# Neighbourhood attention: the values computed with tokens on partitions, four pairs of heads at a time, and the input rounded in column order

## What is computed

```python
for i in range(DEPTH_2):                       # 4 layers
    h = rmsnorm(x, norm1_g[i])
    ...                                        # i == 1: y = nat_mixer(h, ...)
    x = x + y
    h = rmsnorm(x, norm2_g[i])
    x = x + conv_ffn(h, ...)

def nat_mixer(h, w_qkv, q_g, k_g, rpb, w_out):
    rows = s // GRID_W                         # 512 tokens = 8 rows of 64 columns
    qkv = (h @ w_qkv).reshape(b, s, 3, NAT_HEADS, NAT_HEAD_DIM)   # 16 heads of 64
    q = rmsnorm(qkv[:, :, 0], q_g) * (NAT_HEAD_DIM ** -0.5)
    k = rmsnorm(qkv[:, :, 1], k_g)
    v = qkv[:, :, 2]
    # each token attends to all 8 rows of the 16 columns around its own
    ...
    sc = einsum(q, k_win) + bias
    p = softmax(sc)
    out = einsum(p, v_win)
    return out @ w_out
```

## Time and profile before

| | us |
|---|---|
| median of 3 runs | 3117.59 |
| lowest and highest | 3113.52, 3118.71 |
| the profiled execution, its own time | 3118.01 |
| its span in the trace | 3116.2 |
| PE busy in it | 3090.2 |
| POOL, DVE, ACT busy | 1495.0, 1412.7, 1268.6 |

### The profile page before, as it was taken

The page is one execution under the profiler, slowest core; times in us unless marked ns, Lnnn a source line. Parts: engine busy times, 40 slices in busy tenths (PEclk is TensorE's granted clock), DMA queues, the critical chain, the costliest instruction groups (busy, mean ns, idle before and its releaser), DMA issues.

```text
span 3116.2 us, 35743 instructions
## 1 busy us (share of the span) xinstructions
PE 3090.2 (99%) x14233; PEld 2461.1 (79%) x14233; DVE 1412.7 (45%) x2644; ACT 1268.6 (41%) x1973; POOL 1495.0 (48%) x732
## 2 busy tenths in 40 slices
PE   9999999999999999999999999999999999999999
PEld 6768888875888887778888888888888887588887
DVE  6564111288533345445343544423534358763433
ACT  5463222266433335554333333323433337643432
POOL 2225545566454453334554534444454557545554
PEclk9999999999999999999999999999999999999999
DMA  5213333344232333222323322222333335423332
GB/s 191 71 51 92 96 98 97 96 123 128 82 101 94 95 101 105 92 83 94 102 88 101 108 76 80 81 82 75 94 102 95 95 98 136 112 90 102 91 98 88
DMA packets 90038, 302.78 MB, mean 97 GB/s; under 512 B 10000, under 2 KB 10512, under 8 KB 89744
## 3 DMA queue, kind: packets, MB, share of 16 engines
q1 hardware_dynamic: 89152, 299.35, 31.6%
q10 hardware_dynamic: 720, 1.14, 0.1%
HBM read 281.07 MB, written 2.10 MB: 91 GB/s over the span
## 4 chain that ended last, share of the span: by engine, by line
PE 89%; DVE 7%; ACT 2%; DMA 1%; issue 1%; SPq 0%; ACTq 0%; DVEq 0%
PE PS L1492 26%; PE PS L1494 26%; PE PS L1493 26%; PE PS L1701 1%; DVE XH L2129 1%; DVE XL L2131 1%; PE PS L1515 1%; PE PS L1505 1%; PE PS L1506 1%; PE PS L1504 1%; DMA PT<-PD 1%; PE PS L1519 1%; DVE X L2157 1%; DVE PS L2434 1%; PE PS L1571 1%
## 5 line engine op out<-in xcount | busy, mean ns | idle before, releaser
L2597 POOL TENSOR_TENSOR WL<-RAW,WH 128x1024 fp32r<-128x1024 f32 x502 | 1209.6, 2411 | 1236.1 <-ACT WH L1812 1235.8
L1492 PE MATMUL PS<-XH,WH 128*128 128x512 f32 x2632 | 1054.1, 400 | 2.8 <-POOL WL L2597 1.3
L1494 PE MATMUL PS<-XH,WL 128*128 128x512 f32 x2632 | 1027.2, 390 | 0.0
L1493 PE MATMUL PS<-XL,WH 128*128 128x512 f32 x2632 | 1026.8, 390 | 0.0
L1812 ACT ACTIVATE WH<-RAW 128x1024 fp32r<-128x1024 f32 x502 | 527.5, 1051 | 445.5 <-PE PS L1494 433.4
L1492 PEld LDWEIGHTS PS<-XH,WH 128*128 128x128 f32 x2632 | 494.7, 188 | 139.1 <-issue 36.5
L1493 PEld LDWEIGHTS PS<-XL,WH 128*128 128x128 f32 x2632 | 495.1, 188 | 106.6 <-issue 8.9
L1494 PEld LDWEIGHTS PS<-XH,WL 128*128 128x128 f32 x2632 | 494.8, 188 | 104.5
L1492 PE MATMUL PS<-HH,WH 128*128 128x512 f32 x1264 | 495.1, 392 | 4.4 <-DVE HL L2477 4.4
L1494 PE MATMUL PS<-HH,WL 128*128 128x512 f32 x1264 | 493.6, 391 | 0.0
L1493 PE MATMUL PS<-HL,WH 128*128 128x512 f32 x1264 | 493.5, 390 | 0.0
(11 more groups left out here) (278 smaller groups left out, 2378.4 us busy)
## 6 DMA issues: line engine op xcount, KB each, us to landing
RAW<-wst SPq DMA_DIRECT2D x502, 512.0 KB, 3.5
PT<-PD SPq DMA_DIRECT2D x36, 260.0 KB, 4.9
BI<-natb SPq DMA_DIRECT2D x16, 384.0 KB, 4.4
PT<-PD SPq DMA_DIRECT2D x16, 258.0 KB, 4.9
X<-xin SPq DMA_DIRECT2D x16, 256.0 KB, 5.0
PT<-PD SPq DMA_DIRECT2D x8, 262.0 KB, 4.8
X<-cmpw SPq DMA_DIRECT2D x1, 2048.0 KB, 8.1
out<-X SPq DMA_DIRECT2D x8, 256.0 KB, 2.0
```

The lines of the kernel that those rows point to most:

```text
L1492: e.matmul(o, wh, h, start=first, stop=False)
L1493: e.matmul(o, wh, l, start=False, stop=False)
L1494: t = e.matmul(o, wl, h, start=False, stop=last)
L2597: e.tensor_tensor(WL[:, b % NSPLIT, :], RAW[:, b % NRAW, :], WH[:, b % NSPLIT, :].bitcast(f32), SUB).then_inc(*did(lo_made, ("lo", b)))
```

## The change

Three things change in the program.

1. The weights of the attention's first product are stored in another order: v of four pairs of heads, then q and k of these four, then the same for the other four. v is made by `by_tokens` straight with tokens on partitions (8 input chunks times 4 token blocks, twice). DVE scales the four results by 1/rms, which is now a number per partition (`nat_tokens`); these numbers come from 1/rms by 4 transposes once (`rs_tokens`). The three blocks shifted by 64 are put together by two transfers each inside SBUF, 12 transfers in all. The transposes of v and their ACT copies are gone, as is the strided read in `scaled`.
2. For layer 1, `norm_chunk` puts the tokens in column order when it rounds x: it reads X with a stride of 64 numbers, on DVE for XH and XL and on ACT for the square, and writes in order.
3. `norm_stats` is now a queued piece of work, due 8 tiles into the first product. The beats are due 9, 12, 15, 18 and 21 tiles after k. Scores and probabilities lie in PT, not in TT.

```diff
-            out.append(("nat_qkv", 8, 24))
+            for half in range(2):
+                out.append((f"nat_v{half}", 8, 4))
+                out.append((f"nat_qk{half}", 8, 8))
...
-                turned = Ring([PT[:, i, j, :] for i in range(2) for j in range(4)], (*pt_free[0], *pt_free[1]))
+                spread = Ring([PT[:, 0, j, :] for j in range(4)], pt_free[0])
+                turned = Ring([PT[:, 1, j, :] for j in range(4)], pt_free[1])
+                rt = G8[:, 4:8]
+
+                def start():
+                    norm_stats(norm)
+
+                    def turn():
+                        bank = banks.get()
+                        i = step("rs_tokens", norm["rs"].ap, norm["rs_made"], rt, bank.ap, bank.free)
+                        bank.done((i, "rt"))
+                        st["rt"] = (i, "rt")
+                    later(turn, 6, first=True)
+
+                def to_values(t, bank, made):
+                    v = tiles.get()
+                    i = step("nat_tokens", v.ap, bank.ap, rt[:, t:t + 1], (made, st["rt"], *v.free))
+                    bank.done((i, "v"))
+                    cur["v0"].append((v, (i, "v")))
+                    if t == 0:
+                        return
+                    s = tiles.get()
+                    (above, above_made), (below, below_made) = cur["v0"][t - 1:t + 1]
+                    event = ("shifted", cur["half"])
+                    fetch(s.ap[0:64, :], above.ap[64:128, :], shift_in, event, above_made, *s.free)
+                    fetch(s.ap[64:128, :], below.ap[0:64, :], shift_in, event, below_made)
+                    cur["v1"].append(s)
...
-                    i = step("scaled", columns(b.ap), by_column(bank.ap), by_column(norm["rs"].ap),
-                             (made, norm["rs_made"], *b.free))
-                    bank.done((i, "z"))
-                    norm["z"] = z = (i, "z")
+                    norm["z"] = z = scaled(b.ap, bank, norm, made, b.free)
...
-                    def go():
-                        tokens(b.ap, 4, v0)
-                        b.done((tokens(b.ap[:, 64:448], 3, v1), "tr"))
-                    later(go, first=True)
...
-                        ss = tiles.get(), tiles.get()
+                        ss = spread.get(), spread.get()
...
-                        later(beat(n), 4 + 4 * n)
-
-                linear(norm["mv"], 24, evac, mid=lambda: norm_stats(norm), pace=1)
+                        later(beat(n), 9 + 3 * n)
+
+                for half in range(2):
+                    if half == 0:
+                        later(start, 8, first=True)
+                    cur.update(half=half, v0=[], v1=[])
+                    by_tokens(norm["mv"], to_values)
+                    linear(norm["mv"], 8, evac, pace=1, room=4)
...
-            def norm_chunk(i, k, gain, x_made, s, s_free, sq, total):
-                x = X[:, k, :]
+            def norm_chunk(i, k, by_col, gain, x_made, s, s_free, sq, total):
+                x, xh, xl = X[:, k, :], XH[:, k, :], XL[:, k, :]
+                if by_col:
+                    x, xh, xl = by_column(x), columns(xh), columns(xl)
...
-                e.tensor_scalar(XH[:, k, :], x, gain, None, MUL).then_inc(*did(dve_made, (i, "hi")))
+                e.tensor_scalar(xh, x, gain, None, MUL).then_inc(*did(dve_made, (i, "hi")))
...
+            def nat_tokens(i, v, bank, scale, after):
+                for event in after:
+                    w.wait_ge(*at(event))
+                e.tensor_scalar(v, bank, scale, None, MUL).then_inc(*did(dve_made, (i, "v")))
```

More of the change, by code:

```diff
@@ L1233, in evac @@
                                   *slot_free[h % 4])
-                    if kind < 2:
-                        cur[kind] = (b, head_norm(b, z, G8[:, 2:3] if kind == 0 else pcol("nat_k")))
+                    cur[kind] = (b, head_norm(b, z, G8[:, 2:3] if kind == 0 else pcol("nat_k")))
+                    if kind == 0:
                         return
-                    v0, v1 = tiles.get(), tiles.get()
-                    toks = []
-                    def tokens(src, n, dst):
-                        bank = banks.get()
-                        i = step("to_tokens", src, n, z, dst.ap, dst.free, bank.ap, bank.free)
-                        bank.done((i, "tok"))
-                        toks.append((i, "tok"))
-                        return i
-                    def go():
-                        tokens(b.ap, 4, v0)
-                        b.done((tokens(b.ap[:, 64:448], 3, v1), "tr"))
-                    later(go, first=True)
                     (q, qt), (k, kt) = cur[0], cur[1]
+                    v0, v1 = [x for x, _ in cur["v0"]], cur["v1"]
+                    v_made = (*(x for _, x in cur["v0"]), ("shifted", cur["half"]))
                     flight = {}
-                    blocks = [(v0, 0), (v0, 1)], [(v1, 0), (v1, 1)], [(v1, 1), (v1, 2)], [(v0, 2), (v0, 3)]
+                    blocks = (v0[0], v0[1]), (v1[0], v1[1]), (v1[1], v1[2]), (v0[2], v0[3])
                     def scores(n):
@@ L1479, in walk @@
                     bias_free = ret_layer(norm, n2, bias_free)
-                norm = new_norm("norm1", 8 * (layer + 1)) if layer < 3 else None
+                norm = new_norm("norm1", 8 * (layer + 1), layer == 0) if layer < 3 else None
                 ffn(n2, norm, layer, final=layer == 3)
@@ L1822, in norm_chunk @@
                     w.wait_ge(*at(event))
[L1823 removed]
+                e.activation(columns(s) if by_col else s, by_column(X[:, k, :]) if by_col else X[:, k, :],
+                             ACT.Square).then_inc(*did(act_made, (i, "sq")))
             def first_chunk(i, k, gain, x_in):
@@ L2750 @@
     w = g["nat_w_qkv_2"][0]
-    W["nat_qkv"] = w.reshape(D, 3, 8, 128).transpose(0, 2, 1, 3).reshape(D, 3072)
+    for half in range(2):
+        part = w.reshape(D, 3, 8, 128)[:, :, 4 * half:4 * half + 4]
+        W[f"nat_v{half}"] = part[:, 2].reshape(D, 512)
+        W[f"nat_qk{half}"] = part[:, 0:2].transpose(0, 2, 1, 3).reshape(D, 1024)
     W["nat_out"] = g["nat_w_out_2"][0]
```

32 lines of the change are left out of this document (19 added, 13 removed).

## The result

The changed kernel takes 3136.6 us (median of 6 runs, 3134.7 to 3138.2); the kernel before, in six runs beside it, 3114.9 (3112.9 to 3118.7). The ratio is 1.0066, with a 95% interval from 1.0055 to 1.0077: slower by 21.7 us, where +3.6 was forecast and the range ended at 3128.5. Between the two profiled executions it is 20.2 us (spans of 3136.4 and 3116.2).

A forecast was written before the change was run, and what follows sets the result against it. PE, busy 99% of the span, was taken to bound the kernel. Terms: -5.65 - 0.27 + 6.8 + 1.2 + 1.5 = +3.6 us, so 3121.2 us, range 3114.0 to 3128.5.

The forecast's parts named there:

- Turns, -5.65 us: PE in layer 1: 56 transposes of v go (6.1 us), four for `rs_tokens` come in (0.44 us).
- the 0.27 us for XL of chunk 7: PE's last macs of the first output chunk: the old wait for XL goes, -0.27 us.
- Strided reads, +0.59 us a chunk: DVE's layer 1 norm: XH 0.20 and XL 0.39 us longer, +4.7 us for eight chunks, range 0 to 7.7.
- strides cost nothing: Rival at layer 1's norm, 15%: chain ends at 1185.5, PE waits 2.2 us, -3.2 in all, 3114.4 us.
- PE isn't held: Rival at `norm_stats`, 5%: the sum is ready early and the whole -5.9 us shows, 3111.7 us.
- XH at one number a step, POOL in front of the last sum: Rival at layer 1's norm, 20%: chain ends at 1195.4, PE waits 12.0 us, +9.2 in all, 3126.8 us.
- The wait, +6.8 us: PE at `norm_stats`: reaches it at 1183.4, is held until DVE's chain ends at 1190.2.
- The clock, +1.2 us, at most 1.6: PE behind the wait at `norm_stats`: a stretch at half clock costs +1.2 us, between 0 and 1.6.
- The beats, +1.5 us, at most 4: Layer 1's pairs of heads: tighter beats make PE wait ahead of `values`, +1.5 us for all, range 0 to 4.
- The rival "the beats hold PE": Pairs of heads, 10%: ACT's chain late by 0.5 us at each of 16 `values`, 8 us, +10.1 in all, 3127.7.
- "same": Whole kernel's outcome class between faster (below 3111.4 us) and slower (above 3123.8 us), given 0.58.

The follow-up runs named there:

- best1: Changed kernel with layer 1's sums of squares queued 20 products later, second scores ahead of first normalising, and negation on ScalarE: 3112.4 us, ratio 0.9991.
- before_col: Kernel before with only layer 1's rounding of x in column order, q, k and v scaled in plain order: 3123.2 us, ratio 1.0023.
- plain_x: Changed kernel with x for layer 1 rounded in rows' order again, tokens mixed up, only its time read: 3129.7 us, ratio 1.0044.
- neg_act: Changed kernel with the negation of the row maxima done by ScalarE instead of VectorE: 3126.4 us, ratio 1.0033.
- swap: Changed kernel with the second half's scores queued ahead of the first half's normalising inside a beat: 3124.7 us, ratio 1.0030.
- late_swap: Changed kernel with sums of squares queued 20 products later and second scores ahead of first normalising, negation left on VectorE: 3115.8 us, ratio 1.0001.

## Why the prediction was wrong

**Turns, -5.65 us.** Right, as far as it can be told: the transposes are gone, and a kernel without the long waits (best1) shows the gain less what is named above. No run isolates the term. With the 0.27 us for XL of chunk 7, which the prediction takes off too, 0.8 us of best1 stay without a row.

**Strided reads, +0.59 us a chunk.** Right: XH 0.49 to 0.72 (+0.23), XL 0.75 to 1.15 (+0.40), together 0.63. XH kept its double rate. The chain's end was forecast at 1190.2 and came at 1190.5. The rivals "strides cost nothing" and "PE isn't held" fall. The slower one, "XH at one number a step, POOL in front of the last sum", falls in both its parts. before_col pays the same chain at another instruction, so the term belongs to the chain, not to `norm_stats`. One reading was a little off: the prediction has PE meet the chain twice in the kernel before, but its `norm_stats` starts at PE's own pace, 0.23 us behind the matmul ahead of it, and isn't held.

**The wait, +6.8 us.** Near: 6.0 us. The sum came 0.3 us later than forecast, but PE reached the matmul at 1184.5 and not at 1183.4. Of this 0.7 us is a wait for a weight block at 1175.55, some 9 us ahead, so that the two waits come to 6.7. The prediction has the roundings of weight blocks come later behind the slower squares, and puts this at nothing because PE is held anyway; it isn't held yet at that point. plain_x, whose squares are as short as before, doesn't have this wait.

**The clock, +1.2 us, at most 1.6.** Wrong in size: 2.5 us at the boundary, and 3.2 more behind waits in the pairs. The bound was taken from one stretch behind a wait of 2.19 us as if it were the most that could come. Here the low stretch was longer, with part of it on the wait itself, and the prediction had no row for that; it should have kept the upper end open, above all as the wait it forecast was three times as long. The length of one wait doesn't decide it alone: before_col has a mean clock of 0.53 over 7 us with waits of 1.58 and 2.09 us.

**The beats, +1.5 us, at most 4.** This is the step that failed. The waits are 14.3 us and the two low stretches behind them 3.2: 17.5. PE's side of the count was right: it comes to `values` 10.55 us behind the scores, where 10.5 was forecast. ACT's side was not: the first half of the copies, forecast at 10.6, is there at 12.4 in the changed kernel. In neg_act, without the hold, it is there at 11.0. So the hold is most of the miss and not all of it: neg_act still waits 5.4 us in the pairs, over the 4 at which the range ended. What the count left out is that every duration in it came from one pair of the kernel before, in which DVE and POOL don't meet. Moving the beats by five steps and taking a third of the steps out of a pair moved them against POOL's list, and the 0.17 us that the sign takes there became 2.05.

**The rival "the beats hold PE"** named the right place, ACT's chain late ahead of `values`, but not what makes it late, and had the wrong size and the wrong reason against it. It had 0.5 us at 16 `values`, each lateness repaid by the next beat; in fact it is 1.8 us on average at 8, since the second `values` of a pair stand behind the first and wait no more. With the 17.5 us in the place of its 8, the prediction's own sum comes to 3137. It got 10%.

Was it there to be seen? Yes, in three places. The trace of the kernel before has the same kind of instruction in layer 0 (line 2177). In layer 1 it has the normalise itself (line 2216): in the last pair of heads, at 1392.93, one of its steps has POOL's subtraction of 1392.91 beside it and takes 2.52 us instead of 0.35 (DVE lines, ns min/median/max, first and last start, forms):

```profile
L2216 DVE TENSOR_SCALAR TT<-TT,SM x64: 345/349/2517, 1207.8 to 1392.9; 128x256 f32<-128x256 f32 x64
...
L2177 DVE TENSOR_SCALAR SM<-SM x24: 168/170/1553, 41.1 to 218.0; 128x2 f32<-128x2 f32 x24
```

And the prediction itself cited the earlier trace rows, where an XH of 0.49 us takes 2.48 beside a subtraction of POOL, and used that only at the boundary. The rule of the Trainium skill that stood beside it ("GPSIMD Engine Reference", "1. Specifications") applies to any VectorE operation that uses two ports, and so to this one; the trace agrees, with 2.05 against 0.17 us.

The forecast had the sign of the change right, but its most likely class ("same", up to 3123.8 by its own bounds) and its range did not hold.

## What to carry to other kernels

When a change moves work of one engine against another's, don't take durations from a pair, a tile or a layer in which the two don't meet. Read the maximum beside the median of every small instruction on the path, and if one is ten times the other, put it into the chain at its maximum and see who would wait. A chain that crosses from engine to engine several times between scores and values should have slack at least as long as the longest hold; where it has not, look first at the order inside a beat (which cost nothing here and gave 13.6 us), then at the engine that does the small step.

## What the runs showed of the hardware

How short an instruction of VectorE is doesn't matter for the hold, only which kind it is. DVE lines of the changed kernel (ns min/median/max). Inside one of POOL's subtractions began 22 of line 2158's instructions, 5 of line 2164's and over 200 of line 2190's, all its forms together:

```profile
L2158 DVE TENSOR_SCALAR XH<-X,PRM x72: 485/489/2665, 256.7 to 2774.3; 128x512 fp32r<-128x512 f32 x72
```

```profile
L2164 DVE TENSOR_TENSOR TT<-TT x63: 674/685/2889, 259.8 to 2775.5; 128x512 f32<-128x512 f32 x63
```

```profile
L2190 DVE TENSOR_TENSOR PD<-PS,TT x178: 683/693/697, 140.3 to 3095.1; 128x512 f32<-128x512 f32 x178
```

With all operands in SBUF, whether one input or two, an operation can last four or five times its length; with an input in PSUM the longest of 178 is 697 ns. The maxima of line 2234, with PSUM among their inputs too, run through a subtraction at 0.42 us. The Trainium skill says so ("SBUF — State Buffer", "Who interferes with whom"): a VectorE instruction with at most one SBUF input, outside the two-port modes, does not contend with GpSimd; one in a two-port mode does, and whichever is issued second is blocked for the whole of the other. The trace agrees: the eight holds of line 2239 end within 0.03 us of the subtraction's end.

A step of 64 numbers in a read from SBUF costs VectorE 0.23 us in 512 numbers for an operation with one input, which keeps its double rate, and 0.40 for one with two. ScalarE pays more, 0.5 us: the squares of this norm are the maximum of the line, the plain ones its median (ACT, ns min/median/max).

```profile
L1849 ACT ACTIVATE TT<-X x72: 632/633/1189, 256.7 to 2774.3; 128x512 f32<-128x512 f32 x72
```

The clock fell to its lower level during a single wait of 6.0 us, some 4 us into it, and also twice behind waits of 2.8 and 1.9 us ahead of `values`; each stretch cost 1.6 us or more. In the kernels whose waits in the pairs stayed under 1.6 us (neg_act, swap, late_swap, best1) it did not fall there. But a wait of a given length doesn't fix it. PE waits 2.19 us in every kernel behind layer 0's convolution. Over the 12 us from there the granted clock is 0.86 in the changed kernel (774 to 786) as in the kernel before, and 1.00 in best1 (772 to 784), whose instructions are those of the changed kernel up to there. The wait of 2.2 us in plain_x, too, has a clock of 1.00 around it (1180 to 1195). What decides it was not tried. A difference of 1.6 us at one place between two profiled executions can be this and nothing else.
